# Squares, small block and tail of an eight-core encoder step: matmul sums, batches of four, a new order at the handover

## The chip, the cores and the metric

The kernel runs on the eight cores of one Trainium2 chip (cores 0 to 3 on one die, 4 to 7 on the other). No core talks to another. The metric is the device time of the slowest core, in microseconds. Each core has a tensor engine (PE), VectorE (DVE), ScalarE (ACT), GpSimd (POOL) and SyncE (SP), each with its own instruction queue worked off in order; SP and POOL issue the transfers.

## What is computed

One step of an encoder layer for 8 new streams of 2048 frames and 16 running streams of 64 frames. A core has one new and two running streams, 2176 frames of width 1024.

```python
mod = silu(c) @ w_ada + b_ada                       # nine shifts, scales, gates per stream
h = rmsnorm(x, g1) * (1 + sc1) + sh1
x = x + 0.5 * gt1 * swiglu(h, w1_in, w1_out)        # d_ff 2816
h = rmsnorm(x, g_mix) * (1 + sc2) + sh2
z = h @ w_in                                        # q, k, v, forget logits, conv inputs, gates
# forgetting attention: running sums of log f, and a cache of 1024 frames for the running streams
m = sigmoid(ga) * o_attn + sigmoid(gc) * o_conv
x = x + gt2 * (m @ w_out)
h = rmsnorm(x, g2) * (1 + sc3) + sh3
x = x + 0.5 * gt3 * swiglu(h, w2_in, w2_out)
y = rmsnorm(x, g_final)
```

## The kernel before

Activations lie transposed: 128 features by frames. Eight feature tiles k; the frames are cut into four blocks of 512 (tb 0 to 3) and a small block of 128 (tb 4: two streams of 64). x stays in SBUF in float32 (`RX`, tile `xt(k, tb)`), the modulated input of the matmuls in bf16 (`H`), the gated product in `RG`, weights in a ring of eight slots `wsall`. PSUM has eight banks `PB` of 128x512: 0 to 3 take FFN and output products, 4 to 7 the statistics (`stat_bank`), and more for the projections.

A helper writes each instruction and its waits; an engine carries out its own in program order. So the order of the calls is the order of each queue. In the trace all matmuls have line 464 or 462, all ACT operations line 474.

A norm has three steps. Squares: `n_sq` (line 619) writes eight bf16 tiles `SQB` on ACT, or on DVE for odd tiles; `n_sum` (633) writes float32 squares on ACT and POOL adds them one after the other (line 642), the last sum in bf16 `SQS`. Statistics: `n_stats` (647), one matmul with ones on the sum, or eight on the squares, then a logarithm (Ln) and an exponential (Exp) on ACT, the result in the PSUM bank. Modulation: `n_mod` (660), DVE multiplies by scale and statistics into `TW[0 or 1]` (line 667), ACT adds the shift into `H`; for the small block twice per tile, one stream each. `n_final` (675) scales by the last gain and stores y.

*The opening* (first loop after `JB1 = 7`): for each tb, seven groups `ffn_in` j = 0 to 6 (16 matmuls, silu on ACT, product on DVE into RG). `ahead` puts the norm of block tb+1 between them: for tb > 0 squares with POOL sums at j 0 and 1, `n_stats` after j 2, modulations at j 4, 5, 6. At j 3 `sums` scans cached log gates (line 563), whose loads (line 559) stand on SP behind the loads of x. Banks alternate: group n uses banks n%2 and 2 + n%2, so it must find group n-2 evicted.

*Output phases* (`out_phase`, 732): for each block eight products `out_mm` over banks 0 to 3, each evicted by DVE into x with the gate (line 718; the small block twice per product, one stream each). With a `norm`, each eviction is followed by a square, `n_stats` of the block before comes at the product named by `stat_mo`, and its modulations are queued in `modq` and popped two per product (one at every second product of the small block). In the order `MID` = (0, 1, 2, 4, 3) the small block comes before block 3. `out_phase` runs five times: both halves of each FFN, and the projection `w_out` after attention.

*The handover* (line 1450 on): keys, values, `n_stats(3)`, then the modulations of block 3 two per unit between forget-gate matmuls `f_block` (950) and projections. `later(n, fn)` puts off evictions and gate sums by n units. The gate sums are a scan on DVE (line 985), a split into three bf16 rows on POOL (lines 550 to 554), a store `fd` (995) and, after blocks 2 and 4, row loads (1012, 1014) on POOL's queue. Attention reads these rows.

*The tail*: the last FFN output phase takes the blocks in order, so block 3 is normalised during the small block, and the small block after it.

## Time and profile before

| | us |
|---|---|
| median of three runs | 1883.65 (1883.44 to 2082.79) |
| the profiled execution | 1886.12 |
| its span, slowest core (7) | 1884.6 |
| spans of cores 0 to 7 | 1873.5, 1878.4, 1872.8, 1878.2, 1876.4, 1883.7, 1874.8, 1884.6 |

| engine | busy us | share |
|---|---|---|
| PE matmul | 1794.6 | 95% |
| DVE | 764.1 | 41% |
| ACT | 768.6 | 41% |
| POOL | 262.2 | 14% |

The profile is that of core 7. Times in it count from the core's first instruction. The chain that ended last is PE for 84% of the span; DMA, DVE and ACT have 4, 4 and 3%. In the 40 slices PE's digit is 3 and 7 in the first two, 8 in the third and 7 in the last, and 9 in all others; the granted clock is 1.0 or just below in nearly all slices. A timeline row gives start, duration, engine, line, operation, output and input, count and, in brackets, the idle time before it with what ended it.

### The profile page before, as it was taken

The page shows a single profiled execution, that of the slowest core. Times are in us where ns is not written, and L with a number is a line of the kernel's source. Part 1 is how long each engine was busy: PE and PEld are TensorE (multiplying, and loading weights), DVE is VectorE, ACT ScalarE, POOL GpSimd, SP SyncE. Part 2 cuts the span into 40 slices and gives each one's busy share as a digit, 9 for nine tenths or more (in the row PEclk, how much of TensorE's full clock was granted, in tenths as well). Part 3 has the DMA queues.
Part 4 walks back from the last instruction along what each step waited for, and adds up shares of the span by engine and source line. Part 5 has one row for each costly group of instructions (what it writes and reads, how often), then busy time and mean ns, then how long its engine had stood idle before and what let it go on. Part 6 is the DMA issues. An engine that isn't in the chain of part 4 may idle for free.

```text
span 1884.6 us, 35785 instructions; the slowest of 8 cores (1872.8 to 1884.6 us)
## 1 busy us (share of the span) xinstructions
PE 1794.6 (95%) x13248; PEld 957.0 (51%) x13248; DVE 764.1 (41%) x1405; ACT 768.6 (41%) x1492; POOL 262.2 (14%) x337
## 2 busy tenths in 40 slices
PE   3798999999999999999999999999999999999997
PEld 1334545555454565656565656665444444544443
DVE  1333223222268455555555555544652223322255
ACT  2554100111267666666665666665661110011132
POOL 1232100111146300000000000001520000000041
PEclk9988999999999999999999999999999999999998
DMA  9700800897136331313242322233232210422113
GB/s 180 195 4 2 152 12 2 141 162 125 26 146 151 64 83 36 83 36 83 37 94 47 83 51 67 65 120 71 88 57 44 35 29 1 79 34 34 18 59 132
DMA packets 42386, 137.94 MB, mean 73 GB/s; under 512 B 5570, under 2 KB 7972, under 8 KB 39116
## 3 DMA queue, kind: packets, MB, share of 16 engines
q0 software_dynamic: 25456, 81.03, 25.2%
q1 hardware_dynamic: 16760, 54.62, 8.0%
q8 instruction: 110, 1.80, 0.4%
q14 instruction: 60, 0.49, 0.1%
HBM read 180.18 MB, written 36.22 MB: 115 GB/s over the span
## 4 chain that ended last, share of the span: by engine, by line
PE 84%; DMA 4%; DVE 4%; ACT 3%; issue 2%; POOL 2%; DVEq 0%; ACTq 0%; POOLq 0%; SPq 0%
PE pb L464 80%; PE pb L462 4%; DMA RG<-w_ada 2%; DVE tw L667 2%; DMA RX<-xT 1%; ACT H L474 1%; POOL scr L642 1%; ACT scr L474 1%; ACT tw L474 1%; DMA wsall<-w1i 1%; ACT L474 1%; PE pb L1319 0%; ACT RG L474 0%; DVE RX L679 0%; DVE RG L704 0%
## 5 line engine op out<-in xcount | busy, mean ns | idle before, releaser
L464 PE MATMUL pb<-H,wsall 128*128 128x512 bf16 (+1 forms) x5760 | 1159.1, 350 | 26.7 <-ACT H L474 10.8
L464 PEld LDWEIGHTS pb<-H,wsall 128*128 128x128 bf16 x5760 | 513.5, 99 | 525.5 <-issue 51.7
L474 ACT ACTIVATE tw<-pb 128x512 bf16<-128x512 f32 (+3 forms) x320 | 169.3, 532 | 645.7 <-PE pb L464 640.2
L474 ACT ACTIVATE RG<-pb 128x512 bf16<-128x512 f32 (+3 forms) x688 | 345.2, 532 | 174.1 <-PE pb L464 147.3
L464 PE MATMUL pb<-RG,wsall 128*128 128x512 bf16 (+1 forms) x2080 | 388.5, 349 | 0.3
L704 DVE TENSOR_TENSOR RG<-pb,tw 128x512 bf16<-128x512 f32 (+1 forms) x218 | 132.9, 611 | 501.6 <-PE pb L464 444.3
L464 PEld LDWEIGHTS pb<-RG,wsall 128*128 128x128 bf16 x2080 | 186.9, 98 | 199.1 <-issue 5.5
L464 PE MATMUL pb<-RX 68*128 68x512 bf16 (+3 forms) x640 | 214.7, 348 | 1.9 <-ACT RX L474 1.9
L462 PEld LDWEIGHTS pb<-RX,RG 128*128 128x128 bf16 x2176 | 139.0, 97 | 107.1 <-issue 5.8
L718 DVE SCALAR_TENSOR_TENSOR RX<-pb,DER,RX 128x512 f32<-128x512 f32 (+1 forms) x192 | 112.2, 594 | 171.0 <-PE pb L464 167.0
L462 PE MATMUL pb<-RX,RG 128*128 128x65 bf16 x2176 | 169.5, 193 | 2.6 <-ACT RG L474 2.3
L474 ACT ACTIVATE scr<-RX 128x512 f32<-128x512 f32 (+3 forms) x156 | 84.6, 561 | 122.5 <-DVE RX L718 91.6
L642 POOL TENSOR_TENSOR scr<-scr 128x512 f32<-128x512 f32 (+1 forms) x96 | 107.2, 1116 | 180.4 <-ACT scr L474 174.7
L474 ACT ACTIVATE H<-tw,MOD 128x512 bf16<-128x512 f32 (+1 forms) x144 | 85.4, 596 | 60.9 <-DVE tw L667 55.1
L474 ACT ACTIVATE RX<-pb 128x512 f32<-128x512 f32 (+3 forms) x130 | 68.9, 534 | 77.6 <-DVE RX L1132 53.7
L667 DVE SCALAR_TENSOR_TENSOR tw<-RX,DER,pb 128x512 f32<-128x512 f32 (+1 forms) x144 | 84.5, 588 | 28.3 <-ACT pb L474 14.9
L395 POOL DMA_DIRECT2D wsall<-w_in x32 | 17.0, 534 | 438.8 <-PE pb L464 438.8
L464 PE MATMUL pb<-wsall,H 128*128 128x128 bf16 x1088 | 72.8, 220 | 0.0
L464 PEld LDWEIGHTS pb<-wsall,H 128*128 128x128 bf16 x1088 | 66.4, 99 | 7.6 <-issue 1.3
L464 PEld LDWEIGHTS pb<-RX 68*128 68x128 bf16 x640 | 61.6, 97 | 6.8 <-issue 2.1
L1132 DVE CAST RX<-pb 64x512 bf16<-64x512 f32 (+1 forms) x80 | 48.6, 607 | 37.2 <-PE pb L464 30.5
L1151 DVE TENSOR_SCALAR RX<-pb 64x512 bf16<-64x512 f32 (+1 forms) x70 | 42.6, 608 | 39.0 <-PE pb L464 35.0
(106 smaller groups left out, 770.0 us busy)
## 6 DMA issues: line engine op xcount, KB each, us to landing
wsall<-w_in POOLq DMA_DIRECT2D x32, 512.0 KB, 5.6
wsall<-w_ada POOLq DMA_DIRECT2D x28, 512.0 KB, 11.2
wsall<-w1i POOLq DMA_DIRECT2D x22, 512.0 KB, 12.5
wsall<-w2i POOLq DMA_DIRECT2D x22, 512.0 KB, 7.6
RX<-xT SPq DMA_DIRECT2D x4, 2048.0 KB
xs<-RX SPq DMA_DIRECT2D x4, 2048.0 KB
kT<-RX SPq DMA_DIRECT2D x32, 256.0 KB
vo<-RX SPq DMA_DIRECT2D x32, 256.0 KB
```

The lines of the kernel that those rows point to most:

```text
L395: P.dma("gpsimd", lambda e, d=d, s=src: e.dma_start(out=d, in_=s), writes=[WSB[slot]], sem=WSS[slot])
L462: ins = e.matmul(o, lhsT=l, rhs=r, start=st, stop=sp, skip_group_check=True)
L464: ins = e.matmul(o, lhsT=l, rhs=r, start=st, stop=sp)
L474: return P.op("scalar", lambda e: e.activation(out=out, in_=in_, func=func, **kw), reads=reads, writes=writes)
L642: P.op("gpsimd", lambda e: e.tensor_tensor(out=o[:, 0:n], in0=SQF[0][:, 0:n], in1=SQF[i][:, 0:n], op=ALU.add), reads=[B_sqf[0], B_sqf[i]], ...
L667: vec(lambda e, lo=lo, ln_=ln_, seq_=seq_: e.scalar_tensor_tensor(out=TW[i][:, lo:lo + ln_], in0=x_[:, lo:lo + ln_], scalar=der_ap(a_idx, ...
L704: vec(lambda e: e.tensor_tensor(out=gv[:, jj, t0:t0 + n], in0=PB[bb][:, 0:n], in1=SAB[ia][:, 0:n], op=ALU.mult), [PBB[bb], B_sab[ia]], [GB ...
L718: vec(lambda e, lo=lo, ln_=ln_, seq_=seq_: e.scalar_tensor_tensor(out=x_[:, lo:lo + ln_], in0=PB[bank][:, lo:lo + ln_], scalar=gate_ap(mo, ...
L1132: vec(lambda e, hh=hh: e.tensor_copy(out=k_aug[st_][0:64, hh, t0:t0 + n], in_=PB[b][hh * 64:(hh + 1) * 64, 0:n]), [PBB[b]], [B_k[st_][hh][ ...
L1151: vec(lambda e, hh=hh: e.tensor_scalar(out=q_aug[st_][0:64, hh, t0:t0 + n], in0=PB[b][hh * 64:(hh + 1) * 64, 0:n], scalar1=0.125, scalar2= ...
```

## The change

1. *Opening*: blocks 2, 3 and 4 get their squares from `n_sq`, all on ACT, so `n_stats` does eight matmuls. It moves from after j 2 to after j 1, the modulations from j 4, 5, 6 to 3, 4, 5, the cached scan from j 3 to j 0.
2. *Small block in batches*, in all output phases: four products of 128 share a bank, evicted by two DVE operations of 512 (`small_evict`); squares in two ACT operations of 512 (`n_sq4`), statistics in eight matmuls; modulation in three DVE operations of 512 per half (`n_mod4`), none on ACT.
3. *Modulations spread evenly*: over the products that remain, those of the small block left for last. After the first FFN they are popped right behind the phase; after `w_out` in the first FFN group.
4. *Handover*: values and queries move ahead of the forget-gate matmuls of blocks 3 and 4.
5. *Second FFN*: `n_stats(3)` after group 1 instead of 0.
6. *Tail* (`out_tail`): statistics of block 3 go to SBUF (`TW[0]`); three of its eight products run on POOL with the gain on ACT, five on DVE, all before the small block's evictions; stores of two tiles.

```diff
@@ norms
+        SQ4 = [(SQS[1], B_sqs[1]), (LNT[:, 0:256].bitcast(BF16), B_lnt)]
+        X4 = [RX[:, XOFF[4] + 512 * h:XOFF[4] + 512 * (h + 1)] for h in range(2)]
+        def n_sq4(h):
+            act(SQ4[h][0], X4[h], AF.Square, [XB[4 * h + q][4] for q in range(4)], [SQ4[h][1]])
...
-        def n_stats(tb):
+        def n_stats(tb, dst=None):
...
+            if tb in batched:
+                mm([(PB[bank][:, 0:n], ones_bf[:], SQ4[k // 4][0][:, (k % 4) * 128:(k % 4 + 1) * 128],
+                     k == 0, k == 7) for k in range(8)], [SQ4[0][1], SQ4[1][1], B_const], [PBB[bank]])
...
+            if dst is not None:
+                act(dst[0][:, 0:n], LNT[:, 0:n], AF.Exp, [B_lnt], [dst[1]], scale=-0.5)
+                return
...
+        def n_mod4(h, a_idx, sh_kind):
...
+            vec(lambda e: e.tensor_tensor(
+                out=tw4, in0=X4[h].rearrange("p (k t) -> p k t", k=4),
+                in1=PB[bank][:, 0:128].unsqueeze(1).to_broadcast([128, 4, 128]), op=ALU.mult),
+                [PBB[bank]] + [XB[4 * h + q][4] for q in range(4)], [B_tw[i]])
+            vec(lambda e: e.tensor_tensor(out=four(TW[i][:, :]), in0=four(TW[i][:, :]),
+                                          in1=seq_bc(derv[:, a_idx, :, :], h), op=ALU.mult),
+                [B_tw[i], B_der[a_idx]], [B_tw[i]])
+            vec(lambda e: e.tensor_tensor(
+                out=H[:, 4 * h:4 * h + 4, NPR:NT].rearrange("p k (s t) -> p k s t", s=2), in0=four(TW[i][:, :]),
+                in1=seq_bc(modv[:, sh_kind * 8:sh_kind * 8 + 8, :], h), op=ALU.add),
+                [B_tw[i], B_mod[sh_kind]], [HB[4 * h + q][4] for q in range(4)])
+        def n_final_sb(eng, tb, k, rs):
...
+            if eng == "gpsimd":
+                P.op(eng, lambda e: e.tensor_tensor(out=x_, in0=x_, in1=rs[0][:, 0:n], op=ALU.mult),
+                     reads=[XB[k][tb], rs[1]], writes=[XB[k][tb]])
+                return lambda: act(x_, x_, AF.Identity, [XB[k][tb], B_g3], [XB[k][tb]], scale=g3v[:, 3, k, 0:1])
@@ output phases
+        def small_evict(h, bank, gate4, gate_buf, tmp, b_tmp):
+            vec(lambda e: e.tensor_tensor(out=four(tmp), in0=four(PB[bank][:, :]), in1=seq_bc(gate4, h),
+                                          op=ALU.mult), [PBB[bank], gate_buf], [b_tmp])
+            vec(lambda e: e.tensor_tensor(out=X4[h], in0=tmp, in1=X4[h], op=ALU.add),
                [b_tmp] + [XB[4 * h + q][4] for q in range(4)], [XB[4 * h + q][4] for q in range(4)])
+        def out_small(wt, nk, rhs, rb, gate4, gate_buf, norm, prev):
+            for h in range(2):
+                bank = cnt["out"] % 4
+                cnt["out"] += 1
+                for q in range(4):
+                    small_mm(h, q, bank, wt, nk, rhs, rb)
...
+                if norm is not None and h == 0:
+                    n_stats(prev)
+                    modq.extend([lambda k=k: norm(prev, k) for k in range(8)])
+                small_evict(h, bank, gate4, gate_buf, TW[i][:, :], B_tw[i])
+                if norm is not None:
+                    n_sq4(h)
+                    pop_mods(1)
+        def out_tail(wt, nk, rhs, rb, gate4, gate_buf):
+            rs3, rs4 = (TW[0], B_tw[0]), (TW[1], B_tw[1])
...
+            n_stats(3, rs3)
+            gain = [n_final_sb("gpsimd", 3, k, rs3) for k in (5, 6, 7)]
...
+            fin(4)
+            y_store(3, 4, 6)
+            small_evict(0, bank[0], gate4, gate_buf, TW[5][:, :], B_tw[5])
+            gain[2]()
+            y_store(3, 6, 8)
+            n_sq4(0)
+            small_evict(1, bank[1], gate4, gate_buf, TW[5][:, :], B_tw[5])
+            n_sq4(1)
+            n_stats(4, rs4)
+            for k in range(8):
+                n_final_sb("vector", 4, k, rs4)
...
-            sums_at = (0, 1, 2, 3, 4) if order is MID else (0, 1, 2)
+            sums_at = (0, 1, 2, 3) if order is MID else (0, 1, 2)
...
-                    if norm is not None and prev is not None and mo == stat_mo(prev, tb):
+                    if norm is not None and prev is not None and mo == 1:
                         n_stats(prev)
-                        modq.extend([lambda k=k, t=prev: norm(t, k) for k in range(8)])
+                        if prev == 4:
+                            modq.extend([lambda h=h: mod4(h) for h in range(2)])
+                        else:
+                            modq.extend([lambda k=k, t=prev: norm(t, k) for k in range(8)])
...
-                            pop_mods(2 if tb < 4 else mo % 2)
+                            left = max(0, len(modq) - (2 if prev == 4 else 0))
+                            pop_mods(-(-left // (8 - mo)))
@@ opening
         PRE = [[[], [], many("sq", 0, 8), [], many("mod", 0, 2), many("mod", 2, 5), many("mod", 5, 8), []],
-               [many("sq", 0, 4), many("sq", 4, 8), [], [], many("mod", 0, 3), many("mod", 3, 6), many("mod", 6, 8), []]]
+               [many("sq", 0, 4), many("sq", 4, 8), [], many("mod", 0, 3), many("mod", 3, 6), many("mod", 6, 8), [], []]]
...
-                if what == "sq" and tb > 0:
-                    n_sum(tb + 1, k)
-                elif what == "sq":
-                    n_sq(tb + 1, k, k % 2 == 1)
+                if what == "sq":
+                    n_sq(tb + 1, k, tb == 0 and k % 2 == 1)
...
-                if tb < 4 and j == 2:
+                if tb < 4 and j == (2, 1)[tb > 0]:
                     n_stats(tb + 1)
...
-                if tb > 0 and j == 3:
+                if tb > 0 and j == 0:
                     sums[tb - 1]()
@@ handover
+        pop_mods(8)
...
+        run_mods(wrap(v_units(0, 2)) + wrap(q_units(0, 0, True)))
         f_block(3)
-        run_mods(wrap(v_units(0, 2)))
+        run_mods(wrap(q_units(0, 1, True)))
         f_block(4)
-        for tb in (0, 1, 2):
-            run_mods(wrap(q_units(0, tb, True)))
+        run_mods(wrap(q_units(0, 2, True)))
@@ second FFN
-                if tb == 0 and j == 0:
+                if tb == 0 and j == 1:
                     n_stats(3)
```

## Rows read from the trace of the kernel before

**Rows 1.** What PE waited for, whole span: us in total, times, longest

```profile
PE pb L464 <- ACT H L474: 15.2, 5, 4.4
...
PE pb L464 <- POOL tw L642: 10.0, 5, 3.5
```

**Rows 2.** Timeline, opening: start us, us, engine, line, operation [idle before <-releaser]

```profile
79.81 10.52 PE L464 MATMUL pb<-H,wsall 128*128 128x512 bf16 x48 [0.16 <-ACT H L474]
...
81.94 2.19 ACT L474 ACTIVATE scr<-RX 128x512 f32<-128x512 f32 x4 [1.79 <-DMA RX<-xT]
...
89.59 0.88 SPq L559 DMA_DIRECT2D RG<-lfc  x2
...
92.44 1.26 POOL L642 TENSOR_TENSOR tw<-scr 128x512 bf16<-128x512 f32 x1 [0.20 <-POOL scr L642]
...
93.84 0.59 PE L464 MATMUL pb<-tw,ones_bf 128*128 128x512 bf16 x1 [3.51 <-POOL tw L642]
...
94.22 16.50 PE L464 MATMUL pb<-H,wsall 128*128 128x512 bf16 x64
...
94.51 1.28 ACT L474 ACT_TABLE_LOAD   x1 [3.52 <-PE pb L464]
...
106.76 1.59 DVE L667 SCALAR_TENSOR_TENSOR tw<-RX,DER,pb 128x512 f32<-128x512 f32 x2
...
111.28 1.59 DVE L667 SCALAR_TENSOR_TENSOR tw<-RX,DER,pb 128x512 f32<-128x512 f32 x2
...
145.80 12.21 PE L464 MATMUL pb<-H,wsall 128*128 128x512 bf16 x48 [4.02 <-ACT H L474]
...
175.35 11.00 PE L464 MATMUL pb<-H,wsall 128*128 128x128 bf16 x119 [3.47 <-ACT H L474]
```

**Rows 3.** A window of 5 us after the first gap (busy, granted clock, DMA share, GB/s)

```profile
95.00:100.00 5.00, 5.00 (x15) 1.83 (x14) 0.00 (x0) 3.87 (x5) 0.00 (x0) 0.57 0.00 0
```

**Rows 4.** Timeline, matmuls of 128 columns at full clock, tail

```profile
1869.89 1.39 PE L464 MATMUL pb<-RG,wsall 128*128 128x128 bf16 x22
```

**Rows 5.** Chain that ended last: end of the opening (start us, us)

```profile
184.23 30.78 PE pb L464 x199
```

**Rows 6.** Timeline, last row load of the gates

```profile
624.80 0.53 POOL L1012 DMA_DIRECT2D RX<-fd  x1 [1.71 <-DMA fd<-RG]
...
628.38 0.39 PE L464 MATMUL pb<-RX,wsall 68*128 68x64 bf16 x8 [0.80 <-DMA RX<-fd]
```

**Rows 7.** Timeline, handover: logits, scans, a split on POOL, forget matmul

```profile
585.50 0.74 DVE L963 TENSOR_SCALAR RX<-pb,BFt 16x512 f32<-16x512 f32 x1 [1.35 <-PE pb L464]
...
595.22 1.21 DVE L985 TENSOR_TENSOR_SCAN RG<-tw,RG 16x512 f32<-16x512 f32 x1
...
598.95 3.57 PE L464 MATMUL pb<-H,WF 128*16 128x512 bf16 x8 [4.42 <-ACT H L474]
...
599.33 1.51 POOL L554 TENSOR_TENSOR RG<-RX,RG 16x512 bf16<-16x512 f32 x1
...
599.94 1.99 DVE L985 TENSOR_TENSOR_SCAN RG<-tw,RG 16x512 f32<-16x512 f32 x1
```

**Rows 8.** Timeline, projection and the start of the second FFN

```profile
1335.27 1.27 POOL L642 TENSOR_TENSOR scr<-scr 128x512 f32<-128x512 f32 x1 [0.97 <-ACT scr L474]
...
1344.15 0.38 PE L464 MATMUL pb<-tw,ones_bf 128*128 128x512 bf16 x1 [3.24 <-POOL tw L642]
...
1381.50 0.38 PE L464 MATMUL pb<-tw,ones_bf 128*128 128x512 bf16 x1 [1.88 <-POOL tw L642]
...
1391.39 11.40 PE L464 MATMUL pb<-H,wsall 128*128 128x512 bf16 x56 [2.60 <-ACT tw L474]
```

**Rows 9.** Timeline, tail: the last scalings on DVE

```profile
1868.41 0.75 DVE L679 SCALAR_TENSOR_TENSOR RX<-RX,G,pb 128x512 f32<-128x512 f32 x1
...
1873.87 4.40 DVE L679 SCALAR_TENSOR_TENSOR RX<-RX,G,pb 128x512 f32<-128x512 f32 x6
...
1878.74 3.05 DVE L679 SCALAR_TENSOR_TENSOR RX<-RX,G,pb 128x128 f32<-128x128 f32 x7 [0.47 <-DVE RX L679]
```

90 lines of the change are left out of this document (69 added, 21 removed).

## Prediction

> **What bounds the kernel now.** I read the busy shares and the 40 slices first: the tensor engine is busy 95% of the span, so time can come only from its gaps and from stretches at the lower granted clock. The list of what PE waits for [rows 1] names the gaps that this change can touch: waits for the modulated activations H, and for the sums of squares made on POOL. I then laid the timelines of four stretches side by side with the program. The stretch from 184 us to 560 us has no gap, and attention is over 99% busy. So five places remain: the opening (79.8 to 184.2 us), the end of the first FFN half, the handover to attention (580 to 630 us), the projection after attention (1308 to 1405 us), the tail (from 1865 us).
>
> **Opening, part by part.** In a block of 512, PE needs 7 × 16 matmuls at 10.52/48 = 0.219 us, 24.5 us. For the next block, eight squares are made, added on POOL in a chain of about 1.47 us a link, and one matmul follows. In block 1 the squares can't start before x has landed at 81.94, the chain ends at 93.7, and PE stands 3.51 us; H is then late for each of the three blocks that follow, by 4.02 us for block 3 and 3.47 us for the small block [rows 2]. After a gap like these the granted clock is at its lower level, 1.2 GHz, for part of the next 5 us (mean 0.57 [rows 3]): 64 matmuls take 16.50 us instead of 14.0. The gaps of 1.9 and 2.6 us in this trace were followed by full clock, those of 3 us and more were not.
>
> After: ACT alone squares, PE sums with eight matmuls (7 more: 1.53 us in two blocks, 0.4 us for the small one), and the statistics come one group of matmuls sooner. With T as a block's start: squares done T+6.5, statistics T+6.9 to T+8.7, logarithm, exponential and two table loads of 1.28 us let silu 2 end at about T+14.2, modulations start at T+14.9. Three modulations and a silu take 4.52 us (106.76 to 111.28 [rows 2]), so the eighth ends at T+26.2, and the next block wants it at T+26.3. The bank of silu 4 comes about 0.4 us late. So two blocks of 26.3 + 0.6, one of 25.1, and the small block's 112 matmuls at 1.39/22 = 0.063 us [rows 4], 7.1 us: 86.0. Before it was 104.4, from 79.81 [rows 2] to 184.23 [rows 5]. The scan of the cached sums moves from group 3 to group 0 on DVE. Its data are issued on SP only at 89.59, behind the last x blocks [rows 2]; behind the scan stand the product of group 1, whose bank PE wants at about 94.0, and all modulations. Landing by 92.0 costs nothing; a landing of 3.6 us, as the row loads on POOL's queue had (624.80 to 628.38 [rows 6]), costs about 2. I take 1.4. **Opening: −17.0**, bounds −12 (two more late blocks) and −19.5.
>
> **End of the first FFN half.** The small block now leaves two full banks instead of eight quarter ones. The silu and output counters put the next group's first bank (1) on the last half's: PE must wait for one eviction of 512 columns, about 0.75 us by DVE's rows of that size, plus about 0.15. **+0.9**, bounds 0 and 1.6. In the second FFN the same counting lands on a bank that is wanted 1.7 us later: nothing.
>
> **Handover.** Sums inside the phase were hidden before and are after: seven more matmuls of 128 cost 0.4. What ends last here is the modulation of block 3, 4.42 us late [rows 7]. The queries and values moved ahead of that forget-gate matmul give PE about 3.9 us of work, so that wait shrinks. But the small block's modulation is put behind the last eviction, six DVE operations of 512 that depend on each other, about 0.8 each, instead of two pairs: DVE takes up the first forget logits at about 587.5 instead of 585.50 [rows 7]. From there DVE and ACT are a closed chain to 599, so block 3 is also 2.0 late (near 600.8), and so is the first scan, on which POOL's five splits hang. POOL works on them without a rest from the end of that scan, 596.4, until the last store; then come the row loads (624.80), and PE's first cached-attention matmul waits 0.8 us for the last of these [rows 6]. On the other cores this wait is absent, but PE comes there only 1.4 to 2.7 us after the issue, so it is near. The queries' move doesn't shorten this chain. PE arrives about 4.3 us sooner (gap 2.4 instead of 4.42, no slow clock, moved work) and waits for rows that come 2 us later: some 6 to 7 us idle, then the lower clock, about 2.4 by the opening's rows. The end of the wait is what counts: 2.0 late, 0.5 for POOL's last addition against the new DVE operations, 0.4, and 2.4. **+5.3**, bounds +1 (splits faster, clock stays) and +7; if the rows are not awaited at all, −4.7.
>
> **Projection after attention.** Waits on POOL and one on ACT [rows 8]. Two modulations beside one eviction and one square make a link of the chain 0.97 + 1.27 = 2.24 us against PE's 1.73. Spread evenly (one beside each but the first), DVE needs about 1.5 a link. For block 1 I find the chain's end at 1341.5, PE there at 1340.9: 0.6 instead of 3.24, and no slow clock (1.7). Block 2: after only one half of the small block PE waits 1.3 instead of 0.36. The small block's own wait for POOL, about 1, goes with its chain; 0.4 of matmuls is added. So the FFN starts 4.2 sooner. There the statistics of block 3 come one group later and cost no wait (1.88 before), yet the batched modulation now holds DVE six operations, and the silu of block 1 waits for two more modulations: gaps of about 1.8, 0.4 and 2.6, 4.8 in all against 4.7 before. The small block's evictions and modulations are otherwise free. **−5.2**, bounds −8 and −1.
>
> **Tail.** Before, DVE is the path from 1868.41 to 1881.8 [rows 9]; the small block's squares and statistics lie beneath the scaling of block 3. After: five scalings at 0.85 from 1868.41 [rows 9], two pairs of 1.6, then squares, statistics, logarithm, exponential (2.65, now bare), eight small scalings at 0.45: 1882.1, and 0.5 less for the last store, as its forerunners are gone: −0.2. But three block-3 products move to POOL, and DVE's factor moves from PSUM to SBUF. In this trace a DVE scan with two SBUF operands took 1.21 us alone and 1.99 beside a POOL product, which took 1.51 [rows 7]: they take turns. DVE's scaling would give way three times, 1.1 each. I take +2.5 in all. **+2.5**, bounds −1 and +3.5.
>
> The Trainium skill, "SBUF — State Buffer", section "Who interferes with whom", says that GpSimd and VectorE share a port pair under an exclusive lock held for a whole instruction, which an instruction of DVE with two SBUF inputs needs and one with a PSUM input doesn't. By it the tail would be +3.1, without it −0.2. The scan above agrees with it; the additions beside PSUM evictions, 1.27 throughout, do too.
>
> **Sum.** −17.0 + 0.9 + 5.3 − 5.2 + 2.5 = −13.5. The profiled execution has 1886.1 us (span 1884.6 and 1.5 around it), which gives 1872.6. It lies 2.5 above the median of the runs, so for the median: 1870.1. The slowest core's opening gains most (its x lands late), others 3 to 5 us less, and they are 6 to 12 us shorter in span, so it stays the slowest.
>
> **Rivals.** (1) *The handover pays as meant*: rows land before PE needs them. For it: only 0.8 us is waited on one core, 0 on seven. Against it: POOL's unbroken row of splits, on every core. It would give −4.7 instead of +5.3: 1860. Chance 0.17. (2) *Opening and projection are filled less*: the modulations run at the rate of PE with no slack, and one late landing of the cached sums passes into every later block; opening −12, projection −1: 1879. Chance 0.15. (3) *Slower than before*: DVE held by the late landing. The scan stands ahead of the products that free PE's banks; PE's wait grows one for one from a landing after 92.0, and squares for the next block follow only behind the silus. Before, the opening's gaps are worth 17 us here; a landing some 14 us late, at 106, would eat all of it, and only beyond it decides. The small loads after x never show so much. 1885 or more: 0.02. (4) *The opening's change does nothing*, because the eight added matmuls and late H cancel it: the matmuls cost 3.5, the gaps and slow clock 18, so for this H would have to be 3 us later than worked out in each block: 1884, 0.03. (5) *All goes well*: opening −19.5, handover −4.7, projection −7: 1856, 0.05. My forecast: 0.58, its own range 1864 to 1876.
>
> **How the numbers follow.** Two per cent of 1883.65 is 37.7 us, about what a measurement of this kernel can tell from no change. Faster than 1846 would need twice the opening's whole gain beside all the others: 0.03. Slower than 1921: 0.01. Within: 0.96. Range for 8 in 10: 1858 (most of the first rival) to 1879 (the second).
>
> **What would show it.** The opening's end (before 184.2) near 167, granted clock full from 80 on. Squares' matmul without a POOL wait. At the handover the wait for H at block 3's forget matmul down to 2 to 3 us and a new wait for the row loads of 5 to 7. In the projection one wait for POOL of about 0.6, one of 1.3. In the tail, POOL and DVE alternating after 1868 (on before's clock), the last DVE operation not earlier than before relative to the last large matmul. I would be wrong if POOL's splits start as early as before, if a new wait for the cached sums appears near 90, or if gaps remain at the block borders.

## The result, and the profile after

The changed kernel has a median of 1872.04 us (1870.72 to 1873.19, four runs); its ratio to the kernel before is 0.9939, 95% interval 0.9915 to 0.9963. The profiled execution has 1873.19 us, its spans on cores 0 to 7 are 1871.6, 1871.5, 1870.6, 1864.7, 1867.5, 1864.2, 1864.8, 1866.3. The page is now that of core 0; core 7, the slowest before, is among the shorter ones.

The best view of the result is a table by stage. The borders are PE's: the first statistics matmul, the starts and ends of the output phases, the first matmul on the cached keys, the end of the span. All numbers but those of the second row are means over the eight cores of one profiled execution.

| stage, us | before | after | opening alone | all but the opening |
|---|---|---|---|---|
| first statistics to first output half | 221.4 | 207.0 | 206.9 | 224.2 |
| the same, shortest and longest core | 217.2, 227.0 | 204.2, 210.1 | 204.9, 209.5 | 219.2, 227.0 |
| end of first to start of second output half | 171.3 | 172.8 | 171.6 | 172.9 |
| second output half | 82.0 | 83.0 | 82.0 | 83.0 |
| handover, to the first cached-key matmul | 47.6 | 53.1 | 47.8 | 53.6 |
| projection after attention | 68.3 | 63.8 | 67.2 | 63.6 |
| second FFN to its first output half | 167.8 | 167.6 | 168.2 | 167.1 |
| tail, from the last output half | 98.0 | 99.3 | 98.1 | 99.3 |
| whole span | 1877.8 | 1867.6 | 1862.8 | 1885.1 |

Attention (679.5) and the first output half (81.0) didn't move. The opening gives 14.4 us and the projection 4.5; the other stages give back 9. On the mean of the cores that makes 10 us; the slowest span fell by 13.0.

What PE waited for after the change, on core 0 (us in total, times, longest), answers [rows 1]:

```profile
PE pb L464 <- ACT RX L474: 7.6, 5, 3.0
...
PE pb L464 <- ACT H L474: 3.1, 1, 3.1
...
PE pb L464 <- POOL tw L642: 3.1, 3, 1.4
...
PE pb L464 <- DVE RG L760: 2.2, 3, 1.4
...
PE pb L464 <- DVE tw L794: 0.9, 1, 0.9
...
PE pb L464 <- DVE tw L701: 0.8, 1, 0.8
```

The evictions by ACT in the same list before, on core 7:

```profile
PE pb L464 <- ACT RX L474: 2.3, 2, 1.9
```

The waits for H fell from 15.2 to 3.1, those for POOL's sums from 10.0 to 3.1. The waits for ACT's evictions (RX) rose from 2.3 in two pieces to 7.6 in five; all five lie in the handover. The last two lines are new, and DVE's product (L760) has 2.2 where it had 0.2. Line numbers have moved: 985 is now 1111, 963 is 1089, 978 is 1104, 667 is 682, 679 is 727.

The opening in the timeline (start, duration, engine, line, operation, idle before and releaser), for [rows 2]:

```profile
81.29 2.19 ACT L474 ACTIVATE scr<-RX 128x512 bf16<-128x512 f32 x4 [0.43 <-DMA RX<-xT]
...
88.63 1.89 PE L464 MATMUL pb<-scr,ones_bf 128*128 128x512 bf16 x8
...
91.10 0.89 SPq L559 DMA_DIRECT2D RG<-lfc  x2
...
95.11 1.21 DVE L563 TENSOR_TENSOR_SCAN RG<-tw,RG 16x512 f32<-16x512 f32 x1 [8.91 <-DMA RG<-lfc]
...
97.06 2.32 PE L464 MATMUL pb<-H,wsall 128*128 128x512 bf16 x10 [1.36 <-DVE RG L760]
...
116.40 1.89 PE L464 MATMUL pb<-scr,ones_bf 128*128 128x512 bf16 x8
```

The second matmul of squares needs no wait. The scan waited 8.91 us on DVE for its data, and PE 1.36 us for the product behind it. The next statistics stand 27.8 us later and those of the small block 26.2 after them: from there PE runs through. Before, these distances were 33.3 and 30.7 on core 7 and 30.4 and 30.7 on core 1. The wait for the product (L760) is on five of the eight cores, 1.0 to 1.9 us.

The handover, for [rows 7] and [rows 6]. DVE's third and fourth forget gates, POOL's splits, and PE:

```profile
586.67 1.89 PE L464 MATMUL pb<-H,WF 128*16 128x512 bf16 x8 [3.10 <-ACT H L474]
...
590.95 1.21 DVE L1104 SCALAR_TENSOR_TENSOR RG<-RX 16x512 f32<-16x512 f32 x1
...
592.26 1.44 DVE L1111 TENSOR_TENSOR_SCAN RG<-tw,RG 16x512 f32<-16x512 f32 x1
...
594.34 0.73 DVE L1089 TENSOR_SCALAR RG<-pb,BFt 16x512 f32<-16x512 f32 x1
...
595.80 0.60 POOL L550 CAST RG<-RG 16x512 bf16<-16x512 f32 x1
...
598.33 0.68 DVE L1104 SCALAR_TENSOR_TENSOR RG<-RG 16x512 f32<-16x512 f32 x1 [3.01 <-ACT RG L474]
...
602.55 0.60 POOL L550 CAST RG<-RG 16x512 bf16<-16x512 f32 x1
...
609.76 0.58 PE L464 MATMUL pb<-RX 68*128 68x512 bf16 x1 [3.04 <-ACT RX L474]
...
612.45 0.53 POOL L1138 DMA_DIRECT2D RX<-fd  x1 [1.69 <-DMA fd<-RG]
```

The same part of the kernel before shows another order on DVE:

```profile
603.34 0.74 DVE L963 TENSOR_SCALAR RG<-pb,BFt 16x512 f32<-16x512 f32 x1
...
604.00 0.67 DVE L978 SCALAR_TENSOR_TENSOR RG<-RX 16x512 f32<-16x512 f32 x1
...
604.78 1.45 DVE L985 TENSOR_TENSOR_SCAN RG<-tw,RG 16x512 f32<-16x512 f32 x1
```

Before, the logits of block 3 (L963) came ahead of the sums of block 2 (L978, L985). After, they come behind them (L1104, L1111, then L1089): 30.0 us after the end of the output phase instead of 23.5. The granted clock of core 0 then falls by its windows of 5 us (busy us of PE, PEld, DVE, ACT, POOL, then the clock, the DMA share, GB/s):

```profile
600.00:605.00 5.00, 3.19 (x25) 1.59 (x22) 4.52 (x10) 2.81 (x6) 3.89 (x7) 1.00 0.10 19
...
605.00:610.00 5.00, 1.96 (x15) 1.06 (x14) 0.78 (x2) 4.21 (x9) 3.55 (x7) 0.87 0.44 143
...
610.00:615.00 5.00, 5.00 (x23) 2.38 (x22) 0.00 (x0) 1.53 (x4) 3.02 (x5) 0.50 0.04 8
...
615.00:620.00 5.00, 5.00 (x58) 3.05 (x56) 1.20 (x4) 3.47 (x8) 3.21 (x3) 0.94 0.71 115
```

A clock of 0.50 is the lower level, 1.2 GHz; PE had been busy 3.19 and 1.96 us in the two windows before. In the kernel before it stays 1.00 in all five windows from 605 to 630, but it was lower earlier in the same stage, behind the wait of 4.42 us (core 7):

```profile
595.00:600.00 5.00, 1.05 (x3) 0.40 (x4) 4.62 (x8) 3.94 (x7) 2.94 (x4) 0.77 1.02 192
...
600.00:605.00 5.00, 5.00 (x35) 3.10 (x34) 4.76 (x6) 2.60 (x5) 4.08 (x5) 0.55 1.08 246
```

So the low stretch has moved rather than been added: what the clock took from the handover (one minus the granted clock, times the length, an estimate from the clock of all cores) is 3.2 us before and 3.6 after. What grew is PE's idle time in the stage, from 6.6 to 10.7 us on the mean.

The projection and the start of the second FFN, for [rows 8]:

```profile
1331.61 0.38 PE L464 MATMUL pb<-tw,ones_bf 128*128 128x512 bf16 x1 [0.94 <-POOL tw L642]
...
1345.54 0.38 PE L464 MATMUL pb<-tw,ones_bf 128*128 128x512 bf16 x1 [1.41 <-POOL tw L642]
...
1376.32 7.80 PE L464 MATMUL pb<-H,wsall 128*128 128x512 bf16 x40 [0.33 <-ACT tw L474]
...
1387.12 13.19 PE L464 MATMUL pb<-H,wsall 128*128 128x128 bf16 x65 [2.20 <-ACT tw L474]
```

Two waits for POOL, 0.94 and 1.41, where the kernel before had four with 6.5 us together, the longest 3.24. The tail, for [rows 9]:

```profile
1854.19 6.52 DVE L727 SCALAR_TENSOR_TENSOR RX<-RX,G,tw 128x512 f32<-128x512 f32 x5 [3.62 <-ACT tw L474]
...
1854.23 4.61 POOL L724 TENSOR_TENSOR RX<-RX,tw 128x512 f32<-128x512 f32 x3 [21.33 <-ACT tw L474]
...
1866.46 2.19 DVE L727 SCALAR_TENSOR_TENSOR RX<-RX,G,tw 128x128 f32<-128x128 f32 x8 [2.76 <-ACT tw L474]
```

Five scalings take 6.52 us, and three products of POOL run beside the first three of them.

### The profile page after: what moved, and what is told of

It is laid out like the page before. It is cut to its first block, busy times and chain, and to the rows that moved or that the text cites. A ratio compares the mean times of both kernels' runs of the same rounds, so it can differ in the third digit from the quotient of the medians.

```text
span 1871.6 us, 35425 instructions; the slowest of 8 cores (1864.2 to 1871.6 us)
## 1 busy us (share of the span) xinstructions
PE 1791.8 (96%) x13283; PEld 956.1 (51%) x13283; DVE 756.1 (40%) x1322; ACT 756.6 (40%) x1445; POOL 239.7 (13%) x305
## 4 chain that ended last, share of the span: by engine, by line
PE 89%; DMA 5%; DVE 2%; ACT 2%; issue 2%; POOL 1%; DVEq 0%; ACTq 0%; SPq 0%; POOLq 0%
PE pb L464 84%; PE pb L462 4%; DMA RG<-w_ada 2%; DMA RX<-xT 2%; DMA wsall<-w1i 1%; ACT RG L474 1%; PE pb L1445 0%; DVE tw L682 0%; ACT H L474 0%; DVE RX L727 0%; ACT scr L474 0%; ACT tw L474 0%; POOL tw L642 0%; ACT RX L474 0%; DMA RG<-lfc 0%
## 5 line engine op out<-in xcount | busy, mean ns | idle before, releaser
L760 DVE TENSOR_TENSOR RG<-pb,tw 128x512 bf16<-128x512 f32 (+1 forms) x218 | 132.5, 610 | 473.7 <-PE pb L464 430.8
L774 DVE SCALAR_TENSOR_TENSOR RX<-pb,DER,RX 128x512 f32<-128x512 f32 x128 | 96.1, 751 | 173.9 <-PE pb L464 173.8
L474 ACT ACTIVATE scr<-RX 128x512 f32<-128x512 f32 (+2 forms) x132 | 77.4, 607 | 112.9 <-DVE RX L774 102.9
L642 POOL TENSOR_TENSOR scr<-scr 128x512 f32<-128x512 f32 x66 | 83.9, 1272 | 134.9 <-ACT scr L474 132.9
L474 ACT ACTIVATE H<-tw,MOD 128x512 bf16<-128x512 f32 (+1 forms) x112 | 74.5, 668 | 54.8 <-DVE tw L682 50.5
L682 DVE SCALAR_TENSOR_TENSOR tw<-RX,DER,pb 128x512 f32<-128x512 f32 (+1 forms) x112 | 75.6, 675 | 19.1 <-ACT pb L474 11.8
```

The source lines that it names most:

```text
L474: return P.op("scalar", lambda e: e.activation(out=out, in_=in_, func=func, **kw), reads=reads, writes=writes)
L642: P.op("gpsimd", lambda e: e.tensor_tensor(out=o[:, 0:n], in0=SQF[0][:, 0:n], in1=SQF[i][:, 0:n], op=ALU.add), reads=[B_sqf[0], B_sqf[i]], ...
L682: vec(lambda e, lo=lo, ln_=ln_, seq_=seq_: e.scalar_tensor_tensor(out=TW[i][:, lo:lo + ln_], in0=x_[:, lo:lo + ln_], scalar=der_ap(a_idx, ...
L760: vec(lambda e: e.tensor_tensor(out=gv[:, jj, t0:t0 + n], in0=PB[bb][:, 0:n], in1=SAB[ia][:, 0:n], op=ALU.mult), [PBB[bb], B_sab[ia]], [GB ...
L774: vec(lambda e, lo=lo, ln_=ln_, seq_=seq_: e.scalar_tensor_tensor(out=x_[:, lo:lo + ln_], in0=PB[bank][:, lo:lo + ln_], scalar=gate_ap(mo, ...
```

## The experiments

Ratios are to the kernel before, with 95% intervals. Most verdicts rest on the stage table of each profile, means over eight cores; a stage far from an edit moved by about 1 us at most (one exception is named where it occurs), but for the opening, whose mean differs by up to 3 us between executions of the same code.

### The two halves of the change by place

```diff
 opening of the changed kernel, put into the kernel before
-               [many("sq", 0, 4), many("sq", 4, 8), [], [], many("mod", 0, 3), many("mod", 3, 6), many("mod", 6, 8), []]]
+               [many("sq", 0, 4), many("sq", 4, 8), [], many("mod", 0, 3), many("mod", 3, 6), many("mod", 6, 8), [], []]]
...
-                    n_sum(tb + 1, k)
...
-                if tb > 0 and j == 3:
+                if tb > 0 and j == 0:
```

> The kernel before with the change to the opening alone (matmul sums, statistics, modulations and the scan of the cached sums moved up); everything behind it as before. Theory: the opening is worth about 18 us on core 7, whose x lands last (184 to 163 us from the first statistics on in the changed kernel), and 8 to 12 us on the others, and nothing of it is given back behind it, since no later stage waits for anything from the opening. The slowest core's span then falls by 13 to 18 us, to 1867 to 1871. Rival: the scan that stands first on DVE and its late data hold the products, so that the gain of the slowest core is only 8 to 11 us and a wait for DVE's product of 1 to 2 us shows in each of the eight cores.

Measured: 1866.97 us, ratio 0.9895 (0.9855 to 0.9935). The opening is 14.5 us shorter on the mean, all other stages are within 0.4 of before but for the projection (67.2 instead of 68.3). So the opening alone beats the whole change by some 5 us (1866.97 against 1872.04 by the medians, 1862.8 against 1867.6 by the mean spans; the intervals of the two ratios overlap). Its wait on core 1:

```profile
PE pb L464 <- DVE RG L704: 1.3, 1, 1.3
```

The rival's wait is there, 0.9 to 1.4 us on four of the eight cores and none on the others, but it costs just that. The gain of core 7 was 18.8 us (227.0 to 208.2).

The complement is the changed kernel with the old opening:

> The changed kernel with the opening as before (POOL sums, statistics after group 2, scan at group 3). Theory: the stages behind the opening add up on core 7 to +0.9 +0.9 +5.4 -3.9 +1.2 = +4.5 us against the kernel before, as read in the changed kernel's trace, so this one is 3 to 6 us slower than the kernel before. Rival: part of the loss behind the opening comes from the opening's own earlier end (the weights of the next groups and the transfers meet at other times); then this kernel is within 2 us of the kernel before.

Measured: ratio 1.0035 (1.0010 to 1.0059), 6.6 us slower than before with an interval of 2 to 11. Its stages are those of the changed kernel, each within 0.5. The parts add up, and the rest of the change is a loss. In this profile core 3 has the longest opening (227.0), core 7 has 221.6: which core is late changes from one execution to the next. The record bears this out: in the 38 executions of the kernel before that the ratios rest on, each of the eight cores is the slowest at least twice, none more than seven times.

### The handover

Two causes were in dispute: the batched modulations behind the phase, and the new place of the queries. First the old order of the units, with the modulations left where they are:

```diff
-        run_mods(wrap(v_units(0, 2)) + wrap(q_units(0, 0, True)))
         f_block(3)
-        run_mods(wrap(q_units(0, 1, True)))
+        run_mods(wrap(v_units(0, 2)))
         f_block(4)
-        run_mods(wrap(q_units(0, 2, True)))
+        for tb in (0, 1, 2):
+            run_mods(wrap(q_units(0, tb, True)))
```

> The changed kernel with the handover's old order: forget gates of block 3, values, forget gates of block 4, then the queries of blocks 0, 1 and 2. The batched modulation of the small block stays behind the phase. Read from the end of the first FFN to the first matmul on the cached keys, 48.6 us before and 54.0 after on core 7. Theory M (the modulations): six dependent DVE operations before the first forget logits make the whole chain of DVE and ACT late, wherever the queries stand; this kernel needs 52 to 54 us, with a wait for H of 5 to 7 us at the gates of block 3. Theory Q (the queries): their evictions on ACT stand behind the gates' logarithms and those wait for DVE's scans, so PE waits for banks; with the old order PE's waits for ACT's evictions go and the stretch is 49 to 50 us.

Measured: the handover is 50.8 us (53.1 after, 47.6 before); ratio 0.9912 (0.9880 to 0.9944). PE's waits in it, core 1:

```profile
PE pb L464 <- ACT H L474: 6.6, 1, 6.6
...
PE pb L464 <- ACT RX L474: 1.9, 1, 1.9
```

The wait for H is the 6.6 that theory M had, the evictions are down from 7.6 to 1.9 as theory Q had it, and the total lies between both. The row loads are issued 3 to 4 us later than before, and on two cores PE waits for them, 0.5 and 0.6 us. Then the modulations inside the phase, with the new order of the units:

```diff
-                        if prev == 4:
+                        if prev == 4 and nk > 8:
+                            modq.insert(4, lambda: mod4(0))
+                            modq.insert(6, lambda: mod4(1))
...
+                            if prev == 4 and nk > 8:
+                                pop_mods((2, 2, 1, 1, 1, 1, 0)[mo - 1])
+                                continue
```

> The changed kernel with the two batched modulations of the small block put between those of block 2, at the third and the fifth product of block 3, instead of behind the phase (only in the phase ahead of the handover). Theory M: DVE takes up the first forget logits 2 to 3 us sooner, the chain of DVE and ACT with it, and the stretch from the end of the first FFN to the first matmul on the cached keys is 50 to 52 us instead of 54.0. Theory Q: the chain starts sooner but PE still waits for the queries' evictions on ACT, 53 to 54 us. The time inside the phase stays within 1 us under both.

Measured: 50.2 us, with the phase itself unchanged (83.0); ratio 0.9919 (0.9891 to 0.9946). On core 1 the first forget logits start 6.4 us after the phase instead of 8.1, and block 3's forget matmul 19.8 instead of 22.3; the wait for evictions is again 7.6. Each edit alone takes back about half.

Both together, and in the same kernel an edit of the tail (for this one, see below):

> Two stages far apart are edited, each read by itself. Handover: the changed kernel with the old order of the units and the modulations of the small block inside the phase, both edits of the two runs before at once. From the end of the first FFN to the first matmul on the cached keys those needed 50.7 and 50.1 us (median of eight cores), the changed kernel 53.2, the one before 47.6. If the two causes are independent and there is no third, this one needs 47 to 48; if one chain takes both, so that the second undoing brings nothing more, 50. Tail: the statistics of block 3 are written to PSUM for DVE's five scalings and to SBUF for POOL's three, so both engines work on the same tiles at the same time as before, only DVE's factor lies elsewhere. In the changed kernel the five take 6.52 us beside POOL's three of 1.54. If two SBUF operands make DVE give way, they take 4.3 us now, and the tail gets 1 to 2 us shorter (one more exponential on ACT); rival: POOL's traffic alone slows DVE, and they stay above 6 us.

Measured: handover 48.3 us; ratio 0.9896 (0.9873 to 0.9920). The two causes are independent: 53.1 − 50.8 = 2.3 for the order, 53.1 − 50.2 = 2.9 for the modulations, 4.8 for both. Of the 0.7 left against 47.6 a wait of 0.5 for POOL's sum of block 2, which the new phase has, is one part; besides, the row loads are still issued about 1 us later than before, and five cores wait 0.4 to 0.9 us for them.

Is the order's part due to ACT evicting the queries?

```diff
-        run_mods(wrap(v_units(0, 2)) + wrap(q_units(0, 0, True)))
+        run_mods(wrap(v_units(0, 2)) + wrap(q_units(0, 0)))
...
-                if tb > 0 and j == 0:
+                if tb > 0 and j == 3:
                     sums[tb - 1]()
```

> Two stages far apart are edited. Handover: the changed kernel with its new order of units, but DVE evicts the queries of blocks 0, 1 and 2 (ACT in both kernels). Theory Q in the narrow form (evictions of the queries on ACT stand behind logarithms that wait for DVE's scans): PE's five waits for ACT, 7.6 us in all, shrink to 2 to 4 us and the stretch goes from 53.2 to 50 to 51. Rival: DVE and ACT wait for each other in turn, and two conversions of 0.7 us more on DVE for each of three blocks hold the gates' sums as long as ACT is relieved: 53 us or more. Opening: the scan of the cached sums goes back to group 3, everything else there stays new. If the late data of the first scan cost the changed kernel its wait for DVE's product of 1.0 to 1.9 us in the first block after them, that wait is gone and the stretch from the first statistics to the first output half, 207.4 us, falls by 1 to 3 us; the rival says that x itself is late there, and nothing changes.

Measured: handover 55.8 us, so it is worse by 2.7; ratio 0.9965 (0.9951 to 0.9980). The narrow form of theory Q falls. It is work on DVE that lengthens the chain: the logits of block 3 start at 31.6 us, those of the changed kernel at 30.0. The second edit, in the opening, also went against its expectation, both ways. With the scan back at group 3 the opening is 210.4, not shorter but 3.4 longer (little more than the spread of this stage, but steadier by block): its statistics stand 27.2 to 27.6 us apart instead of 26.2. PE's waits there, core 0:

```profile
PE pb L464 <- ACT tw L474: 2.9, 3, 1.4
```

Three waits for a silu: at group 3 the scan stands on DVE ahead of the modulations, ACT's shifts come later, and the silu behind them too. So the scan's move is worth 1.1 us or more in each block, against 1.4 once for its late data.

The last one of the handover starts from the mixed kernel (below), which has the old order, and moves the values alone:

```diff
+        run_mods(wrap(v_units(0, 2)))
         f_block(3)
-        run_mods(wrap(v_units(0, 2)))
         f_block(4)
```

> The mixed kernel with one edit: in the handover the values of blocks 8 to 11 stand ahead of the forget-gate matmul of block 3, the queries where they were. PE has 3.9 us of work in front of its wait for H (4.4 us). If the end of the handover is set by the chain of DVE, ACT and POOL (gate logits, scans, splits), PE only waits later: the stretch stays 47.7 us, or gets 0.5 to 1 longer as the values' eviction stands ahead of the logits on DVE. Rival: PE's own idle time is what counts, and the stretch falls to 44 to 45 us.

Measured: 48.9 us instead of 47.9 in the mixed kernel; ratio 0.9876 (0.9849 to 0.9903). PE gets work in front of its longest wait and the handover gets longer. DVE on core 1:

```profile
587.80 1.49 DVE L1137 SCALAR_TENSOR_TENSOR RG<-RX 16x512 f32<-16x512 f32 x1
...
589.39 1.44 DVE L1144 TENSOR_TENSOR_SCAN RG<-tw,RG 16x512 f32<-16x512 f32 x1
...
591.47 0.73 DVE L1122 TENSOR_SCALAR RG<-pb,BFt 16x512 f32<-16x512 f32 x1
...
594.47 0.85 DVE L1137 SCALAR_TENSOR_TENSOR RG<-RG 16x512 f32<-16x512 f32 x1 [2.01 <-ACT RG L474]
```

The sums of block 2 (L1137, L1144) again stand ahead of the logits of block 3 (L1122), which start 27.2 us after the phase instead of 23.5; DVE then idles 2.01 us for ACT's logarithm. The code says why: `later(4, sums)` counts units. Before, the four ticks after `f_block(2)` are two of the keys and two of the values; at the first tick of the values `later(1, logits)` of block 3 is already due, and it is queued first. With the values ahead of `f_block(3)` the sums are due before that block's logits exist. What this edit costs is 1.0 of the 2.3 us that the whole order costs; how the rest splits among the queries was not tested, and neither was the plain remedy, the old order of the two callbacks with the units moved.

### The tail and the banks

In the kernel with both handover edits undone, the tail's statistics of block 3 were written twice, to PSUM for DVE and to SBUF for POOL:

```diff
             if dst is not None:
+                act(PB[bank][:, 0:n], LNT[:, 0:n], AF.Exp, [B_lnt], [PBB[bank]], scale=-0.5)
                 act(dst[0][:, 0:n], LNT[:, 0:n], AF.Exp, [B_lnt], [dst[1]], scale=-0.5)
...
-            fin = lambda k: n_final_sb("vector", 3, k, rs3)
+            fin = lambda k: n_final_sb("vector", 3, k, (PB[nbank[3]], PBB[nbank[3]]))
```

```profile
1849.64 4.15 DVE L728 SCALAR_TENSOR_TENSOR RX<-RX,G,pb 128x512 f32<-128x512 f32 x5 [3.59 <-ACT pb L474]
...
1850.23 4.09 POOL L725 TENSOR_TENSOR RX<-RX,tw 128x512 f32<-128x512 f32 x3 [21.85 <-ACT tw L474]
```

The five scalings take 4.15 us instead of 6.52, while POOL's three products run at the same time as before and are quicker too, 4.09 instead of 4.61. One by one the trace has 1.85, 1.75 and 1.75 us for the three scalings beside POOL in the changed kernel and 0.74 for the two behind it; here all five have 0.75. The tail is 97.1 instead of 99.3. What made DVE give way is its second operand in SBUF, not POOL's traffic. The Trainium skill, "SBUF — State Buffer", section "Who interferes with whom", says that the port pair that both share is an exclusive lock, that outside its two-port modes DVE needs it only for a second SBUF input, and that the engine that comes second stands until the other's instruction is done. This pair of runs agrees with it.

Next, all eight scalings on DVE, the small block's work between the fourth and the fifth; and another start of the output banks:

```diff
+                    if nk > 8 and norm is None:
+                        cnt["out"] += 1
                     out_small(wt, nk, rhs, rb(4), gate4, gate_buf, norm, prev)
...
-            gain = [n_final_sb("gpsimd", 3, k, rs3) for k in (5, 6, 7)]
...
-            gain[1]()
-            fin(4)
-            y_store(3, 4, 6)
             small_evict(0, bank[0], gate4, gate_buf, TW[5][:, :], B_tw[5])
...
             n_stats(4, rs4)
+            fin(4)
+            fin(5)
+            y_store(3, 4, 6)
+            fin(6)
+            fin(7)
```

> Two stages far apart are edited. Bank: in the first output half the small block takes banks 1 and 2 instead of 0 and 1, so the next FFN group finds bank 1 evicted earlier. The stretch from the first half's end to the second half, 171.3 us before and 172.7 after, falls back to 171.3 to 171.8 if the wait for the eviction (0.9 us) and what follows it was all; it stays above 172.3 if the eight matmuls' order or the clock is behind it. Tail: all eight scalings of block 3 on DVE, none on POOL, and the small block's evictions, squares and statistics between the fourth and the fifth, so that its statistics lie beneath the last four. If turns with POOL and the bare statistics are what the changed tail lost, the tail (99.3 us; 98.0 before) becomes 96.5 to 97.5: eight scalings at 0.85, four operations of 0.75 to 0.8 and eight of 0.28 make 12.1 us on DVE against 14.5. Rival: the stores behind the last scalings set the end, and it stays at 98 to 99.

Measured: ratio 0.9936 (0.9916 to 0.9955). The tail is 95.5 us, 3.8 less than after and 1 us under what was expected. From the mixed kernel, which has the same tail:

```profile
1847.89 2.74 DVE L727 SCALAR_TENSOR_TENSOR RX<-RX,G,tw 128x512 f32<-128x512 f32 x4 [3.62 <-ACT tw L474]
...
1853.53 5.03 DVE L727 SCALAR_TENSOR_TENSOR RX<-RX,G,tw 128x512 f32<-128x512 f32 x12
```

Four scalings with both operands in SBUF take 2.74 us when POOL is quiet; with the factor in PSUM five took 4.15. A single one has about 0.75 us in the trace in either form. The difference is when the next one starts: 0.66 us after it with SBUF, (2.74 − 0.75)/3, and 0.85 with PSUM, (4.15 − 0.75)/4. So the SBUF operand is the quicker one, as long as POOL rests.

The bank edit took the stretch between the output halves from 172.8 to 172.3 and not to 171.3. The edit also met the second FFN, which wasn't meant: there the stretch to the last output half rose from 161.6 to 163.0. The count of banks fits all four cases. In the last small block before a row of FFN groups, banks 0 and 1 cost 1.4 to 1.5 us (first FFN after; second FFN here), banks 1 and 2 cost 1.0 (first FFN here), banks 2 and 3 nothing (second FFN after). What PE waits for in the second FFN here, core 6:

```profile
PE pb L464 <- DVE tw L794: 1.2, 1, 1.2
```

### A mixed kernel

New opening; the output halves of the first FFN and the handover as before (`out_phase_tiles` is the old `out_phase`); new projection; the tail of the last experiment.

```diff
+            if name == "w1o":
+                out_phase_tiles(wt, 11, lambda q, t0, n: gv[:, q, t0:t0 + n], rb_, g_, B_der[gh_idx], norm, after_x,
+                                order)
+            else:
+                out_phase(wt, 11, lambda q, t0, n: gv[:, q, t0:t0 + n], rb_, g_, B_der[gh_idx],
+                          derv[:, gh_idx, :, :], norm, after_x, order, mod4)
```

> New opening, new projection after attention with batches and even spreading, new start of the second FFN; both output halves of the first FFN and the handover as before; the tail with all scalings on DVE and the statistics of the small block beneath them. If the stages add up without interaction, this is the new opening alone (1866.97 us) less some 3 to 4 us for the projection and 1 for the tail: 1862 to 1864 us, a ratio of 0.988 to the kernel before. If the gain in the projection comes only together with the changed handover, 1866.

Measured: 1861.49 us, ratio 0.9872 (0.9855 to 0.9889). It beats the kernel before by 24 us and the changed one by some 10. Handover 47.9, projection 63.3, tail 95.4: the stages add up, and the time is at the lower edge of what was expected.

### Which part of the opening, which part of the projection

Matmul sums alone, with statistics, modulations and scan at their old places, in the kernel before:

```diff
-                if what == "sq" and tb > 0:
-                    n_sum(tb + 1, k)
-                elif what == "sq":
-                    n_sq(tb + 1, k, k % 2 == 1)
+                if what == "sq":
+                    n_sq(tb + 1, k, tb == 0 and k % 2 == 1)
```

> The kernel before with one half of the opening's change: PE sums the squares with eight matmuls; statistics, modulations and the scan stay at their old places. From the first statistics to the first output half the kernel before needs 221.2 us (median of eight cores), with the whole change 206.7. The stall for POOL's sums (3.5 us and the lower clock behind it, 2.5) goes, 3.5 us of matmuls come, and H is still late at the borders of the blocks, 3.5 to 4 us each with the lower clock: 217 to 221 by theory B (both halves are needed, since a late H is set by the places of the modulations). By the rival (ACT and POOL holding each other's buffers made everything late) H comes in time once POOL is out, and this half alone gives 208 to 211.

Measured: ratio 1.0007 (0.9976 to 1.0038), the opening is 225.5 us: nothing gained, 4 lost, somewhat more than theory B had, and little more than the spread of this stage. H is as late as ever, core 1:

```profile
PE pb L464 <- ACT H L474: 11.5, 3, 4.0
```

(In its profile cores 4 and 5 have 27 us more than the others in the second FFN; the opening is not touched by that.) The other half alone, the new places with POOL's sums:

```diff
-               [many("sq", 0, 4), many("sq", 4, 8), [], [], many("mod", 0, 3), many("mod", 3, 6), many("mod", 6, 8), []]]
+               [many("sq", 0, 4), many("sq", 4, 8), [], many("mod", 0, 3), many("mod", 3, 6), many("mod", 6, 8), [], []]]
...
-                if tb < 4 and j == 2:
+                if tb < 4 and j == (2, 1)[tb > 0]:
                     n_stats(tb + 1)
...
-                if tb > 0 and j == 3:
+                if tb > 0 and j == 0:
                     sums[tb - 1]()
```

> The kernel before with the other half: statistics after group 1, modulations at groups 3 to 5, scan at group 0, while POOL still adds the squares in its chain. Theory B: PE comes to the statistics 3.5 us earlier and POOL's sum no earlier, so each block has a wait for POOL of 3 to 7 us in place of the one for H, with the lower clock behind it: 220 to 227 us against 221.2 before, no gain or a loss. Rival: as ACT gets to its modulations earlier, the waits add up to less than the late H did, 212 to 217.

Measured: ratio 1.0083 (1.0061 to 1.0106), the opening is 241.5 us, 20 longer. Theory B had the direction, and missed the size by far. Core 1:

```profile
92.02 1.21 DVE L563 TENSOR_TENSOR_SCAN RG<-tw,RG 16x512 f32<-16x512 f32 x1 [9.24 <-DMA RG<-lfc]
...
93.80 0.60 POOL L550 CAST RG<-RG 16x512 bf16<-16x512 f32 x1 [8.98 <-DVE RG L563]
...
97.91 1.26 POOL L642 TENSOR_TENSOR scr<-scr 128x512 f32<-128x512 f32 x1 [0.20 <-POOL RG L554]
...
103.72 0.59 PE L464 MATMUL pb<-tw,ones_bf 128*128 128x512 bf16 x1 [20.10 <-POOL tw L642]
```

PE waits 20.1 us. POOL's queue has the split of the cached sums (L550) in the middle of its additions (L642); the split waits for the scan, the scan for its data. Since the scan moved along, this run doesn't price the places of statistics and modulations by themselves; it shows that the scan can only be early where POOL has no sums to make. The halves are worth −4 and −20 us, together +14.4: each needs the other.

The projection, in the mixed kernel, tile by tile as before but with even spreading:

```diff
-                            pop_mods(2 if tb < 4 else mo % 2)
+                            if nk == 8 and tb < 4:
+                                pop_mods(-(-len(modq) // (8 - mo)))
+                            else:
+                                pop_mods(2 if tb < 4 else mo % 2)
```

> The mixed kernel with the projection after attention tile by tile as before (small block by single products, sums on POOL, its modulations on DVE and ACT), but with the modulations spread evenly over the products that remain. Before 68.4 us for the projection, in the mixed kernel 62.8 (64.3 in the changed one). If the even spreading is what pays there, 63.5 to 65 us; if the batches are, 67 to 68. The FFN groups behind it, 167.8 us, may take up to 1 us of it back.

Measured: projection 62.5 us (63.3 with batches), ratio 0.9896 (0.9864 to 0.9927). The FFN behind takes 1.1 back (168.4 instead of 167.3), so the two stages together are even, and the last FFN stretch is 163.0, as six more counts of the output bank bring its small block to banks 0 and 1. Even spreading is what pays; the batches bring nothing in the projection.

## Why the prediction was right or wrong

The time, 1872.04 us against 1870.1, lies in both ranges, and no rival came true. The change is −11.6 us by the medians and −13.0 by the slowest spans, against −13.5, but part of this is luck, and steps of the prediction failed.

The main one is in the handover. The prediction let PE run ahead to a wait of "some 6 to 7 us" for the row loads and priced 2.4 us of lower clock behind it. The runs show no wait for the rows on any core; in its place PE waits 4.8 to 7.6 us for evictions by ACT, because the new order of the units delays the logits on DVE, and this costs 2.3 us. The other is in the opening, "so it stays the slowest": on core 7 the stretch from block 1 on shrank by 21.2 us instead of 17, and another core was the slowest.

The terms, as predicted and on the mean of the cores; the measured ones sum to −10:

| term | predicted | measured |
|---|---|---|
| opening | −17.0 | −14.4 |
| end of the first FFN half | +0.9 | +1.5 |
| second output half | 0 | +1.0 |
| handover | +5.3 | +5.5 |
| projection and start of the second FFN | −5.2 | −4.7 |
| tail | +2.5 | +1.3 |

**Opening: mechanism right, terms oversized, one step wrong.** The rate of PE in the filled blocks was worked out as 26.3 + 0.6 and is 26.2; no silu bank came late. The third block takes 24.6 instead of 25.1, the small one 6.5 instead of 7.1. The scan was priced at 1.4 and cost 1.36 on core 0, 0.96 on core 1 and nothing on core 7: on core 0 the data landed some 4 us after their issue, near the 3.6 taken from [rows 6]. From block 1's first matmul on, core 7 thus needs 83.7 us and not 87.4. It needed 104.9 before, a gain of 21.2, beyond the bound of 19.5; of the five others whose records are whole, predicted at 12 to 14, four gained 12.5 to 13.9 and core 5 19.4. Cores 5 and 7 had been the two with a wait of 3.5 us for POOL's first sum; the others had at most 1.7.

The step that failed is "so it stays the slowest". Core 7's whole opening went from 227.0 to 204.2, and its span came to the middle. The lateness of one core was read as its property, and it is one of the execution: in the kernel with the old opening core 3 was the late one. The longest opening of the eight fell from 227.0 to 210.1, by 16.9, and in both executions the slowest core is the one that had it. That this comes so near to −17.0 is luck: it is core 7 before against core 0 after, in one execution each.

**End of the first FFN half: right, undersized.** The wait for the eviction is 0.9 on bank 1, as worked out. Another 0.6 comes with it; the bank runs show that it goes with the pair of banks, not how it splits up.

**Second output half: a step missed.** "Sums inside the phase were hidden before and are after" failed. After only one half of the small block PE comes to the statistics of block 2 before POOL's sum is ready, 0.7 us on core 1. The same mechanism was priced in the projection and forgotten here.

**Handover: half of the mechanism right, the size by luck.** Right: DVE takes up the first logits 2.4 us later (8.1 instead of 5.7 us after the phase; 2.0 predicted), block 3's matmul comes 3.2 later, its wait is 3.1 (2.4 predicted), and undoing it gives back 2.9; 2.0 + 0.5 + 0.4, again 2.9, had been put down for this part. Wrong: "waits for rows that come 2 us later: some 6 to 7 us idle". There is no wait for the rows. They are issued 3.1 us later than before (48.7 after the phase), and PE is there 2.3 to 5.4 us after that, since it waited for evictions first. The prediction held that the queries' move "doesn't shorten this chain"; the moves lengthen it, by turning the order of two callbacks on DVE. What it called PE's 4.3 us of earlier arrival never came about. The last term, 2.4 for the lower clock, isn't there either: a window of 5 us at 0.50 is, but the kernel before had its like, and the difference is about 0.4. The term happens to be as large as the 2.3 of the order, which was put at nothing.

**Projection: right.** Waits for POOL of 0.94 and 1.41 (0.6 and 1.3 predicted), gaps of 0.33 and 2.20 at the FFN's start where 1.8, 0.4 and 2.6 were expected. It was argued from the even spreading, and the run by tiles confirms that this is the cause. One reading of rows does not carry over: gaps of 1.9 and 2.6 us were found to be followed by full clock and those of 3 us and more not, but behind the 2.20 here the granted clock is 0.70 in the window from 1385 to 1390 on core 0.

**Tail: right in kind, two terms oversized and one undersized.** The turns with POOL cost three times (6.52 − 4 × 0.66 − 0.75)/3 = 1.0 us against the 1.1 taken from [rows 7]. But the scalings without POOL were put at 0.85 and 0.45 from [rows 9], whose factor lies in PSUM; with the factor in SBUF they follow each other every 0.66 and 0.26. Over five and eight of them that is 1.0 and 1.5 us less. The sum itself gave +3.1, from which 2.5 was taken; with these numbers it gives about +0.4, and 1.3 was measured. Of the rest 0.6 is the last store: it was to end 0.5 sooner, and the span ends 3.0 us behind the last scaling where it ended 2.8 behind it before. The Trainium skill, "Perfetto Trace Analysis", section "Optimizing Scalar/DVE Operations", gives a DVE instruction about 60 ns of access overhead on SBUF and 125 on PSUM, and says that the profiled latency is about twice that. An estimate from these figures is 0.07 us between the two forms, or 0.13 in the latency. The trace agrees in the direction only: both forms have 0.75 us, and they follow each other 0.66 and 0.85 us apart, a difference of 0.19.

The two kernels that undo parts put a price on what the prediction could only sum: the change contains a gain of 14 us that needs no more than the opening, 4.5 in the projection, and 9 us of losses, all from small reorderings on DVE, POOL and the banks.

## What to carry to other kernels

Moving work in front of a wait fills PE only if the queues of the other engines keep their order: write down, for each engine, what the move puts ahead of what, above all where evictions and sums are deferred by a count of units. With a tuned kernel, read a change by stage over all cores and undo it stage by stage; the mixed kernel that came out of that is about twice as far from the start as the change was. A late core in one profile is no late core in the next, so gains are to be taken from the longest of the eight, not from a fixed one.
